# Second experts: token numbers through a table in memory, gathers issued ahead, one transfer per step for the output rows

## The reference, cut to what matters

```
h        = rmsnorm(x)                       # 512 x 1024
group    = argmax softmax(h @ wg + bg)      # 4 groups of 4 experts
two best experts of that group, with weights that sum to the group's probability
u_e      = silu(h @ w_gate[e]) * (h @ w_up[e]) * weight      # 1024 -> 256
y        = sum over the two experts of u_e @ w_down[e]       # 256 -> 1024
out      = rmsnorm(x + y)
```

## Time and profile before

| what | value |
|---|---|
| median of 3 timed runs | 1780.99 us (1780.74 to 1786.05) |
| the profiled execution, its own time | 1787.18 us |
| its span, first to last instruction | 1785.4 us |
| PE busy | 1686.0 us, 94% of the span |
| DVE, ACT, POOL busy | 726.2, 400.8, 22.1 us |
| granted clock of PE, mean | 0.977 of full speed |

### The profile page before, as it was taken

One profiled execution on the slowest core, in us unless ns is written; L12 is line 12 of the kernel. 1 busy time (PEld: TensorE's weight loads), 2 busy tenths in 40 slices (PEclk: granted clock), 3 DMA queues, 4 the chain that ended last, 5 costly groups with the idle time before them and its releaser, 6 DMA issues. The chain is left out here.

```text
span 1785.4 us, 21495 instructions
## 1 busy us (share of the span) xinstructions
PE 1686.0 (94%) x8607; PEld 951.5 (53%) x8607; DVE 726.2 (41%) x1337; ACT 400.8 (22%) x737; POOL 22.1 (1%) x29
## 2 busy tenths in 40 slices
PE   6998999998999999999999989999999999877987
PEld 3576456657886534443444333444478664454543
DVE  4644513656546011111111115974762424351425
ACT  5112112442214101010101031015641023210112
POOL 0000000000000000000000000000000000000001
PEclk9998999999999999999999999999999999988999
DMA  9421157101133999999999970411112231269974
GB/s 364 137 86 47 71 193 278 48 32 67 67 141 118 398 425 423 421 418 426 424 419 419 426 293 0 142 47 48 47 63 80 94 135 77 94 263 381 325 271 177
DMA packets 88934, 374.35 MB, mean 210 GB/s; under 512 B 9796, under 2 KB 10132, under 8 KB 73748
## 3 DMA queue, kind: packets, MB, share of 16 engines
q1 hardware_dynamic: 82084, 350.14, 50.0%
q10 hardware_dynamic: 3712, 12.06, 1.8%
q0 software_dynamic: 3056, 11.01, 1.7%
HBM read 466.51 MB, written 10.49 MB: 267 GB/s over the span
## 5 line engine op out<-in xcount | busy, mean ns | idle before, releaser
L2236 PE MATMUL bank<-H,weight_slots 128*128 128x512 f32 (+1 forms) x704 | 286.3, 565 | 4.1 <-ACT H L808 2.9
L2236 PEld LDWEIGHTS bank<-H,weight_slots 128*128 128x128 f32 x704 | 135.8, 195 | 149.2 <-issue 143.8
L2652 PE MATMUL bank<-weight_slots,SM 128*64 128x512 f32 x640 | 143.9, 595 | 9.4 <-DMA weight_slots<-in_w_up_e 9.4
L2337 PE MATMUL bank<-R,weight_slots 128*128 128x256 f32 x560 | 123.9, 380 | 0.0
L2680 PE MATMUL bank<-weight_slots,SM 128*64 128x512 f32 x384 | 114.6, 609 | 3.6 <-DMA weight_slots<-in_w_down_e 3.6
L2337 PEld LDWEIGHTS bank<-R,weight_slots 128*128 128x128 f32 x560 | 106.1, 190 | 15.7 <-issue 1.5
L2236 PE MATMUL bank<-R 128*128 128x128 f32 (+2 forms) x784 | 104.5, 286 | 9.5 <-DVE R L2088 6.2
L3028 PE MATMUL bank<-weight_slots,SM 128*32 128x256 f32 x1536 | 91.0, 390 | 21.3 <-DMA weight_slots<-in_expert_w_gate 11.5
L2236 PEld LDWEIGHTS bank<-R 128*128 128x128 f32 x784 | 94.4, 195 | 13.4 <-DVE R L2085 6.3
L2652 PEld LDWEIGHTS bank<-weight_slots,SM 128*64 128x64 f32 x640 | 45.4, 137 | 104.2 <-issue 84.1
L1762 DVE TENSOR_TENSOR R<-SM,bank 128x512 f32<-128x512 f32 x16 | 11.0, 687 | 217.7 <-PE bank L2652 217.7
(11 more groups left out here) (513 smaller groups left out, 2101.6 us busy)
## 6 DMA issues: line engine op xcount, KB each, us to landing
weight_slots<-in_expert_w_gate SPq DMA_DIRECT2D x51, 1024.0 KB
weight_slots<-in_expert_w_up SPq DMA_DIRECT2D x51, 1024.0 KB
R<-in_expert_w_down SPq DMA_DIRECT2D x51, 1024.0 KB
weight_slots<-in_w_up_e SPq DMA_DIRECT2D x24, 2048.0 KB, 17.3
weight_slots<-in_w_down_e SPq DMA_DIRECT2D x24, 2048.0 KB, 23.7
weight_slots<-in_w_in SPq DMA_DIRECT2D x18, 2048.0 KB, 9.5
weight_slots<-in_w_gate_e SPq DMA_DIRECT2D x16, 2048.0 KB, 17.0
weight_slots<-in_w_ada SPq DMA_DIRECT2D x12, 2048.0 KB, 10.7
```

Of the source, the lines that this page charges most:

```text
L2236: ins = nc.tensor.matmul(dst, lhsT, rhs, start=(i == 0), stop=(i == len(pairs) - 1))
L2337: ins = nc.tensor.matmul(bank_half(name, i, half)[:, TC * tile:TC * (tile + 1)], lhs[:, kk, m:m + 128], rhs[:, kk, :], start=(begins and k ...
L2652: ins = nc.tensor.matmul(b[64 * half:64 * half + 64, :], xs[:, 4 * rows + k, 64 * e:64 * e + 64], w[k][:, 512 * half:512 * half + 512], st ...
```

## The change

- Row numbers get another layout in memory: row = partition * 12 + step, where it was column by column. `token_slot` is worked out for it by ten DVE instructions, put after `first_rows` and ahead of `block_expert`; the two instructions that made it before go.
- POOL fills a table `id_table` in memory with zeros early. When `token_slot` is there, it issues eight indirect transfers that write all token numbers (4 bytes each) into the table, then the gather of step 1 (whose numbers PE still makes), then waits for the eight, reads the table back in one transfer (128 x 48 bytes), waits for it, and issues the gathers of steps 2 to 11 one after the other, each only held until the gather four before it has landed.
- `find_rows` and `name_rows` of steps 2 to 11 go, on DVE and PE.
- `y_out` issues one transfer of 128 rows in place of four of 32.

The core of the diff:

```diff
-                by_step = y_rows.rearrange("(c q r) d -> q c r d", c=NSLOT, q=NQUAD)
-                for c in range(NSLOT):
-                    act.dma_start(by_step[q, c], ybuf[q % 2][BLK * c:BLK * (c + 1), :]).then_inc(sem(f"y_out{q % 2}"), 16)
+                act.dma_start(y_rows.rearrange("(p q) d -> q p d", q=NQUAD)[q], ybuf[q % 2]).then_inc(sem(f"y_out{q % 2}"), 16)
...
-            nc.vector.tensor_scalar(token_slot[:, 0:TT], pos2[:, 0, :], -1.0, 0.0, ALU.add, ALU.max).then_inc(sem("token_slots"), 1)
...
-            nc.vector.tensor_scalar(token_slot[:, TT:2 * TT], pos2[:, 1, :], -1.0, 0.0, ALU.add, ALU.max).then_inc(sem("token_slots"), 1)
...
+            step(nc.vector.tensor_copy(token_ids[:, :], token_id))
+            step(nc.vector.tensor_scalar(place, pos8, 1.0, None, ALU.max))
+            tt(column_hits..., place..., column_row[:, 1:NSLOT]..., ALU.is_gt)          # 128 x 24
+            step(nc.vector.reduce_sum(in_column, column_hits..., AX_X))
+            step(nc.vector.scalar_tensor_tensor(out=rows_before, in0=in_column, ...))
+            tt(row_hits8..., rows_before..., thresh[:, 1:NQUAD]..., ALU.is_gt)          # 128 x 88
+            step(nc.vector.reduce_sum(rows_before, row_hits8..., AX_X))
+            step(nc.vector.tensor_scalar(rows_before, ...))
+            step(nc.vector.scalar_tensor_tensor(out=place, ...))
+            nc.vector.scalar_tensor_tensor(out=token_slot[:, :], ...).then_inc(sem("token_slots"), 1)
...
             x_turned(0)
-            find_rows(2)
             for q in range(NQUAD):
-                if q + 2 < NQUAD:
-                    name_rows(q + 2)
                 if q + 1 < NQUAD:
                     x_turned(q + 1)
                 hidden(q)
-                if q + 3 < NQUAD:
-                    find_rows(q + 3)
...
+            for q in LATE:
+                nc.gpsimd.dma_start(y_rows.rearrange("(p q) d -> q p d", q=NQUAD)[q], row_zeros).then_inc(sem("rows_blank"), 16)
+            nc.gpsimd.dma_start(id_table.rearrange("(p q) a -> p (q a)", q=NQUAD), row_table[:, :]).then_inc(sem("rows_blank"), 16)
+            pool.wait_ge(sem("rows_blank"), 16 * (len(LATE) + 1))
+            pool.wait_ge(*reached("token_slots", 1))
+            for i in range(2 * TT):
+                nc.gpsimd.indirect_dma_start(id_table, bass.IndirectOffsetOnAxis(ap=token_slot[:, i:i + 1], axis=0), token_ids[:, i % TT:i % TT + 1], None).then_inc(sem("ids_out"), 16)
             pool.wait_ge(sem("h_written"), 16 * TT)
             for q in range(1, NQUAD):
-                pool.wait_ge(sem("row_ids"), q)
+                if q == 1:
+                    pool.wait_ge(sem("row_ids"), 1)
+                if q == 2:
+                    pool.wait_ge(sem("ids_out"), 16 * 2 * TT)
+                    nc.gpsimd.dma_start(row_table[:, :], id_table.rearrange("(p q) a -> p (q a)", q=NQUAD)).then_inc(sem("ids_back"), 16)
+                    pool.wait_ge(sem("ids_back"), 16)
                 if q == 8:
                     pool.wait_ge(sem("q_turn_x"), 2)
+                if q >= 5:
+                    pool.wait_ge(sem(f"rows_in{q % 4}"), 16 * ((q - 4) // 4 + (1 if q % 4 else 0)))
+                ids = row_ids if q == 1 else row_table
...
-            for name, value in (("xtok_v", 2 * TT), ("x_sq", 2 * TT), ("thin_ev", 5), ("g_v", 2), ("token_slots", 2)):
+            for name, value in (("xtok_v", 2 * TT), ("x_sq", 2 * TT), ("thin_ev", 5), ("g_v", 2), ("token_slots", 1)):
                 pe.wait_ge(*reached(name, value))
             pick_rows()
...
                 gate_up(q, 1)
-                if q + 2 < NQUAD:
-                    name_rows(q + 2)
                 if q + 1 < NQUAD:
                     turn_rows(q + 1)
```

More of the change, by code:

```diff
@@ L127 @@
 VECTOR_STAGES = [("gains1", 2), ("u_fold", 12), ("kw_ev", 16), ("gains2", 1), ("shift_logit", 1), ("aff_v", 8), ("gain_both", 1), ("router_w", 1), ("glu_s", 2), ("a_s", 2), ("f_v", 5), ("c_v", 1),
-                 ("xtok_v", 8), ("x_ss", 1), ("x_inverse", 1), ("chosen", 1), ("token_slots", 2), ("first_hits", 3), ("block_tables", 1), ("late_hits", 2), ("late_rows", 2), ("out_sum", 16)]
+                 ("xtok_v", 8), ("x_ss", 1), ("x_inverse", 1), ("chosen", 1), ("first_hits", 3), ("token_slots", 1), ("block_tables", 1), ("late_hits", 2), ("late_rows", 2), ("out_sum", 16)]
 def bases(stages):
@@ L233, in build @@
         row_ids = ctx.enter_context(nc.sbuf_tensor("row_ids", [P, NQUAD], I32))
+        token_ids = ctx.enter_context(nc.sbuf_tensor("token_ids", [P, TT], I32))
+        row_table = ctx.enter_context(nc.sbuf_tensor("row_table", [P, NQUAD], I32))
+        id_table = nc.dram_tensor("id_table", (P * NQUAD, 1), I32, kind="Internal").ap()
         h_rows = nc.dram_tensor("h_rows", (T, D), F32, kind="Internal").ap()
@@ L1232, in y_out @@
                 if q >= 2:
-                    act.wait_ge(sem(f"y_out{q % 2}"), 16 * NSLOT * (q // 2))
+                    act.wait_ge(sem(f"y_out{q % 2}"), 16 * (q // 2))
                 for half in range(2):
@@ L2085, in _ @@
             nc.vector.tensor_tensor(first_rows, first_rows, second_rows, ALU.add).then_inc(sem("first_hits"), 1)
+            place, in_column, rows_before, column_hits, row_hits8 = (R7[:, c:c + n] for c, n in ((2304, 8), (2312, 8), (2320, 8), (2328, 24), (2352, 88)))
+            step(nc.vector.tensor_copy(token_ids[:, :], token_id))
+            step(nc.vector.tensor_scalar(place, pos8, 1.0, None, ALU.max))
+            tt(column_hits.rearrange("p (n c) -> p n c", n=2 * TT), place.unsqueeze(2).broadcast_to([P, 2 * TT, NSLOT - 1]), column_row[:, 1:NSLOT].unsqueeze(1).broadcast_to([P, 2 * TT, NSLOT - 1]), ALU.is_gt)
+            step(nc.vector.reduce_sum(in_column, column_hits.rearrange("p (n c) -> p n c", n=2 * TT), AX_X))
+            step(nc.vector.scalar_tensor_tensor(out=rows_before, in0=in_column, scalar=-float(BLK * NQUAD), in1=place, op0=ALU.mult, op1=ALU.add))
+            tt(row_hits8.rearrange("p (n q) -> p n q", n=2 * TT), rows_before.unsqueeze(2).broadcast_to([P, 2 * TT, NQUAD - 1]), thresh[:, 1:NQUAD].unsqueeze(1).broadcast_to([P, 2 * TT, NQUAD - 1]), ALU.is_gt)
+            step(nc.vector.reduce_sum(rows_before, row_hits8.rearrange("p (n q) -> p n q", n=2 * TT), AX_X))
+            step(nc.vector.tensor_scalar(rows_before, rows_before, -float(BLK * NQUAD - 1), -float(NQUAD), ALU.mult, ALU.add))
+            step(nc.vector.scalar_tensor_tensor(out=place, in0=in_column, scalar=-float(BLK * (NQUAD - 1)), in1=place, op0=ALU.mult, op1=ALU.add))
+            nc.vector.scalar_tensor_tensor(out=token_slot[:, :], in0=place, scalar=float(NQUAD), in1=rows_before, op0=ALU.mult, op1=ALU.add).then_inc(sem("token_slots"), 1)
             by_column = expert_prev.rearrange("a (c q) -> a c q", c=NSLOT)
@@ L2202, in _ @@
             nc.gpsimd.memset(row_zeros, 0.0).then_inc(sem("zeros_by_pool"), 1)
-            pool.wait_ge(sem("zeros_by_pool"), 2)
+            nc.gpsimd.memset(row_table[:, :], 0).then_inc(sem("zeros_by_pool"), 1)
+            pool.wait_ge(sem("zeros_by_pool"), 3)
             pool.wait_ge(sem("h_ready"), 2 * KD)
-            late_part = y_rows.rearrange("(c q r) d -> c (q r) d", c=NSLOT, q=NQUAD)
-            for c in range(NSLOT):
-                nc.gpsimd.dma_start(late_part[c, BLK * LATE[0]:BLK * NQUAD, :], row_zeros[0:2 * BLK, :]).then_inc(sem("rows_blank"), 16)
@@ L2976, in _ @@
             pe.wait_ge(sem("x4"), KD)
-            b = take(2, "token_slots", 2)
+            b = take(2, "token_slots", 1)
             chosen = rt["chosen"].rearrange("p t g j -> p t (g j)")
@@ L3075, in _ @@
                 if q in (9, 10):
-                    pe.wait_ge(sem("row_ids"), NQUAD - 1)
+                    pe.wait_ge(sem("row_ids"), 1)
                     turn_late(q - 9)
```

9 lines of the change are left out of this document (4 added, 5 removed).

## The result

The changed kernel takes 1796.0 us (median of 12 runs, 1788.36 to 1798.84), the kernel before 1786.0 in the same comparison (12 runs, 1780.12 to 1795.42). The ratio is 1.005, with a 95% interval of 1.0032 to 1.0069: about 9 us slower, outside the range given, and on the side that the forecast held for less likely. The profiled execution took 1798.8 us, the slowest of the twelve.

The account below looks back on a forecast made before the run. PE's 21.5 us of weight waits were taken as the bound, with DMA full in steps 1 to 3 and load issue also limiting later. Terms 2.1 + 1.0 - 1.0 + 6.5 + 1.0 - 7.5 - 1.2 = +0.9 gave 1782 us, range 1771 to 1790.

Parts of the forecast that it names:

- Eight scatters ahead of the gather of step 1: POOL before step 1: scatters delay gather 1, so PE waits about +1.0 us, bounds 0 and 2.2.
- a term for the clock (+1.0): Steps 1 to 3: longer waits lower PE's clock, costing 1.0 us.
- Ten DVE instructions, +2.1: DVE ahead of the expert tables: net 2.1 us on the chain, shifting step 0's loads and `pick_rows` together.
- Scatters of 1.24 each: POOL: each scatter takes 0.94 us plus 0.30 to the next, 9.9 for eight; gather 1 issued near 1582.
- The 1.48: POOL beside DVE work: a scatter might take 1.48 us instead of 0.94, 4.3 more if all eight did.
- Table round trip, 0: Before step 2: gather 2 issued between 1590 and 1598, covered by weight waits; 0, without that cover up to 7 us.
- the 1.0 of step 0 and the 2.9 of steps 4 to 9: PE without `name_rows`: -1.0 us in step 0's chain, and three later steps at 0.98, counted within -7.5.
- Gathers in a row, +6.5: Steps 1 to 3, DMA full: six or seven more gathers delay weights by up to 9.3 us; +6.5 taken.
- given back -7.5: Steps 4 to 9: gathers gone and PE shorter recover 7.5 us, bounds -2.9 and -14.7.
- One output transfer, -1.2: After step 9: one issue of output rows instead of four saves 1.2 us, bounds 0 and -1.4.
- a costly burst: Slower rival, steps 1 to 3: gathers cost full bytes, +9.3, and only -4 returns; sum +7.2, 1788; chance 0.16.
- a late gather 1: Slower rival before `turn_rows(1)`: scatters at 1.48 make PE wait 4.3 us more; sum +5.2, 1786; chance 0.08.

Follow-up runs that it names:

- experiment 1: Kernel before plus eight unused 4-byte scatters in the old layout and the read-back, gathers still one per step: 1796.1 us, 1.0052.
- 3: Changed kernel with its gathers of steps 2 to 11 held to one per step; scatters, table and read-back stay: 1791.5 us, 1.0031.
- 8: Kernel before plus eight unused scatters of 64-byte rows instead of 4-byte ones: 1784.8 us, 1.0003.
- 9: Kernel before plus eight unused 4-byte scatters, each number to a place 64 bytes from the next: 1786.2 us, 1.0008.
- 10: Changed kernel with table rows of 64 bytes instead of 4, first words taken out by DVE: 1794.6 us, 1.006.
- 11: Changed kernel with 64-byte table rows, table instructions behind `expert_change`, gather 1 between fourth and fifth scatter: 1798.2 us, 1.0077.
- 13: Changed kernel with 64-byte table rows and the gathers of steps 3 to 11 held to one per step: 1795.5 us, 1.0049.
- 7: Kernel before plus sixteen unused 4-byte scatters, the second eight into a second table, and the read-back: 1798.2 us, 1.0072.
- 16: Changed kernel, 64-byte rows, table instructions behind `expert_change`, gather 1 among scatters, gathers paced, TensorE waiting for `first_hits` instead of `token_slots`: 1798.6 us, 1.0073.
- 4: Kernel before without finding and naming the rows of steps 2 to 11, no table, gathers one per step with step 1's numbers: 1783.8 us, 0.9993.
- 6: Kernel before plus two unused 4-byte scatters instead of eight, and the read-back: 1.0002.
- 12: Kernel before with one transfer of output rows per step: 1784.4 us, 0.9998.
- 15: Changed kernel, 64-byte rows, table instructions behind `expert_change`, gather 1 among the scatters, gathers held to one per step: 1789.3 us, 1.0014.
- 2: Kernel before with gathers of steps 2 to 11 in a row right after gather 1, step 1's row numbers, no scatters: 1785.0 us, 0.9992.
- 5: Changed kernel without scatters and read-back, gathers still in a row with step 1's row numbers: 1789.3 us, 1.0025.
- 17: Changed kernel without scatters and read-back, table instructions behind `expert_change`, TensorE waiting for `first_hits`, gathers in a row: 1793.2 us, 1.0053.
- 14: Kernel before with gathers of steps 2 to 11 in a row only once step 0's rows are turned, no table: 1784.6 us, 0.999.
- 18: Kernel before plus eight unused 4-byte scatters into the dense table behind the gather of step 6, no read-back: 1804.8 us, 1.0118.

## Why the prediction was wrong

**The failed step is the one on the scatters**, "Eight scatters ahead of the gather of step 1", with the one behind it on the table. There a scatter costs what its issue on POOL takes, the one thing that can be late is gather 1, and the table's way is hidden: together +1.0. Step 0 was in the sum with +2.1 + 1.0 - 1.0 = +2.1 in all. In the trace its end came 15.5 us later after the block count (39.4 against 23.9), split so: 2.2 in PE's wait for `pick_rows`, 0.4 in `pick_rows`, 3.3 between its end and step 0, 9.6 within step 0. No term stood for the last two. Of the 9.6, 1.6 are the lower clock of the gate half; the rest lies in the up half, in its pauses and at the lower clock of its end. The sum did have a term for the clock (+1.0), but in steps 1 to 3. I treated step 0 as safe because its weights and rows were there in time, and asked of POOL's transfers only what they do to the weights of steps 1 to 3.

*What is shown.* With scatters under way at the end of `pick_rows` its last signal comes late. By the modelled ends of its matmuls: 3.5 us in the changed kernel, 2.3 and 2.4 in experiments 1 and 3, 2.0, 2.1, 2.7, 1.8 and 2.6 in 8, 9, 10, 11 and 13, 13.0 and 6.6 in 7 and 16. It is 0.3 in the kernel before, 4, 6 and 12, where no indirect transfer is being issued then and DVE is busy until then; only in 15 is it 0.3 in spite of scatters. With gathers there (2, 5, 17) it is 0.9 to 1.6. And step 0's halves take 7.1 us in 3, 4, 8, 9, 12 and 13. They take 8.3, 11.0, 11.3 and 10.6 in 5, 10, 14 and 17, where gathers are issued beside them, at the full clock and with pauses. Gathers beside step 0 don't always do this: in 2 (8.8 us), and in 11 (9.2) for the greater part, the added time is that of a granted clock of one half for 3.4 us. The lower clock also lengthens step 0 to 8.9 in 16 and 9.2 in 7, where no gathers in a row run beside it.

*What isn't.* Why a TensorE that waits for no data pauses while GpSimd issues indirect transfers was not found; the records show "issue" and an unknown queue, and SP held up with it. Every execution here was recorded, so a part of the recording in the pauses isn't ruled out. Each part alone is within 0.1% of before (scatters at such distance 8 and 9, gathers 2 and 14, naming 4, output rows 12), the whole forms are 0.1 to 0.8% above. The ten table instructions were never run alone; they are what 5 and 17 have beyond the parts that cost nothing, but their own price in the trace is 2.2 us, 0.12%. So what the traces show is a late step 0, made up of several small delays, one of them the clock; how the parts add to more than their sum stays open.

**The other steps.**
- *Ten DVE instructions, +2.1*: right. `expert_change` comes 10.4 us after the block count instead of 8.4, and `pick_rows` waits 2.2 more.
- *Scatters of 1.24 each*: right for the issue (0.96 to 1.23 and 0.30). Gather 1 was issued at 1580.5, which is 19.1 us after the block count (forecast 1582, 18.1 after it), and PE did not wait for it; the +1.0 was 0. The 1.48 that was weighed for a scatter beside DVE came in none of the eight (in experiment 1 two took 1.41 and 1.52, without an effect to be seen).
- *Table round trip, 0*: right as to data. Gather 2 was issued at 1587.4, 26.1 us after the block count and so at the early end of the 1590 to 1598 given (26.1 to 34.1), and no step waited for its rows.
- *name_rows*: the 1.0 of step 0 and the 2.9 of steps 4 to 9 don't show alone (4: 1.0 us in the median, within the interval).
- *Gathers in a row, +6.5, clock +1.0, given back -7.5*: weights that come later behind gathers, and steps that give it back, are what experiment 2 shows: +7.7 at step 4 and +0.4 at step 11. The size of the net was right in part by luck: the loss came ahead of step 1 and not in steps 1 to 3, 1.7 of it as the clock of step 0, and nearly all of it came back although `name_rows` stayed, so the 2.9 counted for a shorter PE had no part in it. In the changed kernel steps 1 to 3 took 2.2 us more than before and steps 1 to 9 together 1.4 less. The ten gathers' packets ran from 1589.1 to 1612.4, not to 1646: they moved their 5.24 MB at 225 GB/s. They started beside the long step 0 and not beside steps 1 to 3.
- *One output transfer, -1.2*: 0 (12). The larger transfer lands 6.81 us after the last copy, before it was 1.44 + 5.03 = 6.47. What the issues save the landing takes.
- *Rivals*: the slower ones were on the right side and on the wrong place. Neither a costly burst nor a late gather 1 came. One bound there has a slip: with 0.9 in the sum, burst less recovery must be 4.4 us more, not 3.4, to pass 5.3.

Why a late step 0 is not made good is argued and not shown: the earlier trace rows had DMA shares of 0.97 to 1.00 in steps 1 to 3, and loads wait for slots that PE frees, so they start later by as much. In 2 and 14 step 4 comes 9 to 10 us later than before too and the time doesn't suffer. The row was in the prediction; the question what could make step 0 late beyond its data was missing.

## What to carry to other kernels

Before you move work into memory, ask what the removed work costs by running the kernel without it: here that bound (between 0.24% gained and 0.1% lost) would have settled what there was to win. When transfers move beside a stretch that waits for nothing, price that stretch too, and put it into the sum if full DMA engines stand behind it, since the delay may then stay. Look at the granted clock of such a stretch before you look for another cause. An experiment that adds a part alone must keep its addresses: scatters to the old places measured another cost than the change has.

## What the runs showed of the hardware

1024 writes of 4 bytes to neighbouring places of memory cost 9 us ahead of step 0 (experiment 1), and 21 together with a gather that waits for them (18); the DMA engines then show a share of 0.80 to 1.00 at 120 to 156 GB/s, and the last scatter lands 10.7 and 15.2 us after POOL starts to wait. The same writes 64 bytes apart, or of 64 bytes each, land 2.8 and 2.4 us after POOL starts to wait and cost nothing measurable. The Trainium skill (DMA: Bandwidth & Descriptors, "Specifications") says that transfers below 512 bytes are read, modified and written back by the DMA engine. No row here shows a reading back. The spread and the 64-byte writes are below that size too and cost nothing measurable, so here the distance between writes decides, not the size alone.

TensorE's signals mostly arrived 0.9 to 3.5 us late (6.6 and 13.0 in 16 and 7), and its matmuls paused by 0.3 to 1.0 us, while GpSimd issued indirect transfers, with no wait in the records that accounts for it; a register move on SP took 0.70 us in such a pause and not 0.03.

A granted clock of one half (1.2 GHz) for 3.4 us cost 1.6 to 1.7 us in 64 matmuls: 5.2 us in the changed kernel and 5.35 in experiment 2, 3.66 at the full clock. The idle time of PE ahead of it was 4.3 and 2.4 us; in 3 and 13 the clock stayed full behind 3.1 and 3.4 us of idle time, so the idle time just ahead does not tell it by itself.
